# Query and key columns turned channel by token, their rotary partners swapped by transfers, and top-k rounds respaced

## The reference

```python
h = rmsnorm(x, norm_g)
a_q, a_k, a_v, a_z, i_q, i_k, i_w, b_q, b_k, b_v, b_z, b_o, b_i, b_f, g_a, g_b = split(h @ w_in)
q_a, k_a = partial_rope(a_q), partial_rope(a_k)     # 8 heads of 64 channels, the first 16 rotated
q_i, k_i = partial_rope(i_q), partial_rope(i_k)     # 16 query heads of 64, one key head
# branch a: 64-token chunks; top 128 keys of score = sum_h w_h * relu(q_i[h] . k_i / 8), then softmax attention
# branch b: chunked mLSTM on silu(causal_conv(b_q, b_k)), b_v, gates b_i and b_f, then head norm
x = x + (sigmoid(g_a) * y_a + sigmoid(g_b) * y_b) @ w_out
out = rmsnorm(x, final_norm_g)
# partial_rope: [x1*cos - x2*sin, x1*sin + x2*cos, rest], x1 and x2 the first and second 8 channels of a head
```

## Time and profile before

| | |
|---|---|
| median of 3 runs | 505.21 us (505.19 to 505.41) |
| the profiled execution's own time | 505.35 us |
| its span, first to last instruction | 503.6 us |
| granted TensorE clock, mean | 0.998 of full speed |
| TensorE matmul busy | 494.5 us, 98% |
| VectorE busy | 261.4 us, 52% |
| ScalarE busy | 239.2 us, 47% |
| GpSimd busy | 213.0 us, 42% |

### The profile page before, as it was taken

How to read it: one execution, slowest core, us unless ns; L and a number is a source line. 1 busy time by engine, 2 the same in 40 slices (tenths; PEclk the granted TensorE clock), 3 DMA queues, 4 the chain that set the end, 5 groups by cost and what they waited for, 6 DMA issues and landing times.

```text
span 503.6 us, 6823 instructions
## 1 busy us (share of the span) xinstructions
PE 494.5 (98%) x2518; PEld 411.6 (82%) x2518; DVE 261.4 (52%) x575; ACT 239.2 (47%) x434; POOL 213.0 (42%) x130
## 2 busy tenths in 40 slices
PE   8999999999999999999999999999999999999995
PEld 7688888888888888888788888888888888887885
DVE  3865777877899936525655567531111011125433
ACT  6757655555554455536568652413330333152322
POOL 0675131333344444247487451246534663373000
PEclk9999999999999999999999999999999999999999
DMA  8654432212343243112223112043234426453111
GB/s 284 188 153 128 126 87 79 84 48 80 83 111 99 85 117 104 52 43 85 57 70 85 43 43 65 20 125 104 62 87 125 126 58 193 126 149 144 42 55 72
DMA packets 44841, 48.94 MB, mean 97 GB/s; under 512 B 4996, under 2 KB 30212, under 8 KB 44808
## 3 DMA queue, kind: packets, MB, share of 16 engines
q1 hardware_dynamic: 43944, 47.65, 32.3%
q10 hardware_dynamic: 864, 0.86, 0.5%
HBM read 46.40 MB, written 2.11 MB: 96 GB/s over the span
## 4 chain that ended last, share of the span: by engine, by line
PE 94%; DMA 2%; SPq 1%; POOL 1%; ACT 1%; DVE 1%; issue 1%; DVEq 0%
PE pj L1486 24%; PE pj L1487 24%; PE pj L1488 24%; DMA w_raw<-in_w_in 2%; PE ob L1617 2%; PE tr L1606 2%; PE qb L1554 2%; PE qb L1553 2%; PE ob L1487 1%; PE qb L1487 1%; PE ob L1488 1%; PE qb L1488 1%; PE ob L1486 1%; PE qb L1486 1%; PE tr L1541 1%; PE qb L1601 1%
## 5 line engine op out<-in xcount | busy, mean ns | idle before, releaser
L529 POOL TENSOR_TENSOR w_lo<-w_raw,w_hi 128x1024 fp32r<-128x1024 f32 x70 | 168.9, 2424 | 156.3 <-ACT w_hi L875 156.0
L1486 PE MATMUL pj<-w_hi,h_hi 128*128 128x512 f32 x272 | 109.6, 403 | 0.0
L1488 PE MATMUL pj<-w_hi,h_lo 128*128 128x512 f32 x272 | 106.5, 392 | 0.0
L1487 PE MATMUL pj<-w_lo,h_hi 128*128 128x512 f32 x272 | 106.4, 391 | 0.0
L1486 PE MATMUL pj<-h_hi,w_hi 128*128 128x512 f32 (+1 forms) x200 | 78.1, 390 | 1.0 <-DVE h_lo L1129 1.0
L875 ACT ACTIVATE w_hi<-w_raw 128x1024 fp32r<-128x1024 f32 (+1 forms) x72 | 73.5, 1045 | 9.8 <-DMA w_raw<-in_w_out 6.3
L1488 PE MATMUL pj<-h_hi,w_lo 128*128 128x512 f32 (+1 forms) x200 | 77.9, 389 | 0.0
L1487 PE MATMUL pj<-h_lo,w_hi 128*128 128x512 f32 (+1 forms) x200 | 77.8, 389 | 0.0
L1488 PEld LDWEIGHTS pj<-w_hi,h_lo 128*128 128x128 f32 x272 | 51.1, 188 | 11.4
L1486 PEld LDWEIGHTS pj<-w_hi,h_hi 128*128 128x128 f32 x272 | 51.2, 188 | 8.3 <-issue 0.2
L1487 PEld LDWEIGHTS pj<-w_lo,h_hi 128*128 128x128 f32 x272 | 51.3, 188 | 8.0
(11 more groups left out here) (216 smaller groups left out, 817.3 us busy)
## 6 DMA issues: line engine op xcount, KB each, us to landing
w_raw<-in_w_in SPq DMA_DIRECT2D x60, 512.0 KB, 3.6
w_raw<-in_w_out SPq DMA_DIRECT2D x5, 512.0 KB, 3.5
x_tok<-in_x SPq DMA_DIRECT2D x4, 512.0 KB, 5.3
w_raw<-in_w_branch_a SPq DMA_DIRECT2D x8, 256.0 KB, 2.9
w_raw<-in_w_branch_b SPq DMA_DIRECT2D x8, 256.0 KB, 3.3
x_again<-in_x SPq DMA_DIRECT2D x1, 2048.0 KB, 9.3
w_late<-in_w_out SPq DMA_DIRECT2D x3, 512.0 KB, 6.1
out<-y_norm SPq DMA_DIRECT2D x4, 320.0 KB, 2.3
```

The source lines that it names most:

```text
L529: eng.tensor_tensor(lo[:, 0:m], raw_slot(n)[:, 0:m], hi[:, 0:m].bitcast(F32), ALU.subtract).then_inc(lo_by_dve if n in DVE_SLOTS else lo_b ...
L1486: pe.matmul(bank, a_hi, b_hi, start=first, stop=False)
L1487: pe.matmul(bank, a_hi, b_lo, start=False, stop=False)
L1488: return pe.matmul(bank, a_lo, b_hi, start=False, stop=last)
```

## The change

1. iq0, iq1, aq and ak are computed channel by token, as bq and bk were. The indexer groups have four units of 384 tokens instead of three of 128 tokens by 512 channels. The job `stage_chan` and its transposes are gone; ScalarE copies a unit to `iq_chan`, `q_a` or `k_chan`, and this copy alone frees the bank.
2. Rotation now works on whole channels by tokens. When a group's four units are out, ScalarE issues four transfers that copy rotary rows to their partners' places in `swapped` (`swap`); GpSimd multiplies that by the sines (`sin`), VectorE multiplies the channels by the cosines and adds the two (`turn`), block by block of 128 channels. Then ScalarE and VectorE make the two parts from SBUF (`parts`).
3. The tables come from the rope columns, which ride in `gate_l`, now 128 columns wide, through one transposition of four pieces (gate_rows); ScalarE copies them out four times. Rows are transposed back in four pieces (gate_cols). GpSimd blanks the padding at the start.
4. Scores go head by head, three tiles each. All 48 top-k rounds come after the last score: a round of tile 3 each 4.5 places from 66 on, the pair of tiles 2 and 1 two places behind it, to 135.

Places of the first units are now: iq0 4, iq1 20, aq 36, ak 52, bq 68, bk 84, bv 100, av 116, bo 132. Scores are at 28 to 65, attention starts at 139.

```diff
-UNITS = [("small", 0)] + [(g, j) for g in GROUPS for j in ((3, 2, 1) if g in ("iq0", "iq1") else range(TILES))]
+UNITS = [("small", 0)] + [(g, j) for g in GROUPS for j in range(TILES)]
-SCORES = [(i, h) for i in (3, 2, 1) for h in range(IDX_HEADS)]
+SCORES = [(i, h) for h in range(IDX_HEADS) for i in (3, 2, 1)]
-    return first_quarter("iq1") + 4 + (4 * s) // 5
+    return first_quarter("iq1") + 8 + (4 * s) // 5
...
-    for n, u in enumerate(STAGED):
-        put(4 * UNIT[u] + 4 + 2, "stage_chan", n)
+    for n, g in enumerate(TURNED):
+        end = first[g] + 16
+        put(end, "swap", n)
+        for b in range(KW):
+            put(end + 4 + 3 * b, "sin", 4 * n + b)
+            put(end + 5 + 3 * b, "turn", 4 * n + b)
+            if (g, b) in PARTS:
+                put(end + 6 + 3 * b, "parts", PARTS.index((g, b)))
...
-    start = score_place(IDX_HEADS - 1) + 1
-    place = start
+    start = score_place(len(SCORES) - 1) + 1
     for r in range(ROUNDS):
+        place = start + (9 * r) // 2
         at.setdefault(place, []).append((3, r))
-        place += 4 if first_quarter("ak") <= place < first_quarter("bq") else 2
-    pairs = place
-    for r in range(ROUNDS):
-        at.setdefault(pairs + 3 * r, []).append((2, r))
-        at.setdefault(pairs + 3 * r, []).append((1, r))
+        at.setdefault(place + 2, []).append((2, r))
+        at.setdefault(place + 2, []).append((1, r))
...
+            pool.memset(gate_l[:, :, :], 0.0)
+            pool.memset(two_rows[:, :], 0.0)
+            pool.memset(cos_t[:, :], 1.0)
+            pool.memset(sin_t[:, :], 0.0)
+            pool.memset(swapped[:, :], 0.0).then_inc(blank_made, 1)
...
+                    if job[0] == "sin":
+                        pool.wait_ge(swap_in, 64 * (job[1] // KW + 1))
+                        pool.tensor_tensor(swapped_rows(g, b), swapped_rows(g, b), table(sin_t, g), ALU.mult)\
+                            .then_inc(sin_made, 1)
...
+                elif kind == "swap":
+                    act.wait_ge(unit_out, UNIT[(g, KW - 1)] + 1)
+                    if n:
+                        act.wait_ge(rotated, KW * n)
+                    for first in (0, A_DIM):
+                        low, high = slice(first, first + HALF), slice(first + HALF, first + ROT)
+                        act.dma_start(swapped[low, 0:size], chan_flat(g)[high, :]).then_inc(swap_in, 16)
+                        act.dma_start(swapped[high, 0:size], chan_flat(g)[low, :]).then_inc(swap_in, 16)
+                elif kind == "parts":
+                    act.wait_ge(rotated, KW * TURNED.index(g) + b + 1)
                     for e in range(2):
-                        src, hi, _ = part(job, e)
+                        src, hi, _ = part(n, e)
                         act.activation(hi, src, ACT.Copy).then_inc(part_hi_made, 1)
...
+                elif kind == "turn":
+                    dve.wait_ge(swap_in, 64 * (m // KW + 1))
+                    dve.tensor_tensor(rows_b, rows_b, table(cos_t, g), ALU.mult).then_inc(cos_made, 1)
+                    dve.wait_ge(cos_made, m + 1)
+                    dve.wait_ge(sin_made, m + 1)
+                    dve.tensor_tensor(rows_b, rows_b, swapped_rows(g, b), ALU.add).then_inc(rotated, 1)
...
-                    if s in (0, 8, 24, 40):
-                        wait_read(pe, ("stage_chan", STAGED.index(("iq0" if h < 8 else "iq1", i))))
+                    if i == TILES - 1 and h % 2 == 0:
+                        pe.wait_ge(part_lo_made, h + 2)
...
-                        if g in CHAN_GROUPS:
-                            a, b = w_part(n, c + j * P, c + (j + 1) * P), h_part(k, 0, SEQ)
+                        wide = SEQ - first_token(g)
+                        if g in CHAN_GROUPS + TURNED:
+                            a, b = w_part(n, c + j * P, c + (j + 1) * P), h_part(k, SEQ - wide, SEQ)
-                        ins = three(bank[:, :], a, b, k == 0, k == KT - 1)
+                        ins = three(bank[:, 0:wide], a, b, k == 0, k == KT - 1)
```

207 lines of the change are left out of this document (108 added, 99 removed).

## The result

The changed kernel takes 532.05 us (median of 4 runs, 530.69 to 532.56) against 505.20 before: a ratio of 1.0526, 95% interval 1.0507 to 1.0546. The forecast was 520.5 us, in a range of 510 to 531. So the direction was right, but the time lies 1.05 us above the range, and the loss of 26.8 us is 11.5 larger than forecast. The profiled execution has 532.14 us and a span of 530.3.

A forecast was written before the change was run, and what follows sets the result against it. TensorE, busy 98%, was taken as the bound, with VectorE 95% full in bq and bk. 505.35 - 5.9 (saving) + 3.5 (first score) + 13.3 (queue) + 4.5 (port) = 520.85; forecast 520.5 us, range 510 to 531.

The forecast's parts named there:

- TensorE's saving: Whole TensorE queue: dropped transposes save 6.9 us, 384-column matmuls add 0.6, first unit 0.35; net gain 5.9 us.
- The full queue from the last score to bv: bq to bv: VectorE's fixed queue before unit 24's conv makes bv's second unit start 13.3 us late.
- sign of VectorE busy over 97%: From the last score (place 66) to bv: VectorE would show over 97% busy.
- The port waits: Last score to bv: two-SBUF-source VectorE instructions wait for GpSimd's running instruction; 4.5 us, bounds 0 and 22.
- nine pairs: Last score to bv: two-source instructions of 5 turns and 4 parts, each pair waiting 0.5 us for GpSimd.
- The scores stage: First score and the seven places after it: TensorE waits 3.5 us together, bounds 0.5 and 8.
- The first part of the term: First score: TensorE waits 2.8 us for swap transfers, GpSimd's remainder, sine product, sum and parts.
- another 0.7: Seven places after the first score: three turns, three parts and ten scores on VectorE cost 0.7 us more.
- rival D: TensorE's clock falls in the waits, mostly hidden in the stretch, three units not hidden; 524 to 537 us; chance 0.15.
- Rival B: VectorE's queue is the bound; port waits and first score cost almost nothing; 512.6 us, 510 to 513; chance 0.14.
- C: Faster: conv does not hold unit starts, as VectorE works ahead or rounds find gaps; 499.3 us; chance 0.10.

The follow-up runs named there:

- e14: Changed kernel without the rotation (swaps, sine products, turns) and without the top-k rounds; 501.16 us.
- e1: Changed kernel without all 96 top-k rounds, masks made from the raw scores; 523.96 us.
- e6: Changed kernel without top-k rounds, each turn's two two-source VectorE operations replaced by maxima of one SBUF source; 512.63 us.
- e17: Changed kernel without top-k rounds, swap transfers and sine products; each turn keeps two full-width one-source VectorE maxima; 506.66 us.
- e11: Changed kernel with GpSimd doing the whole rotation of aq and ak, every 4 places instead of 3; 533.67 us.
- e12: Changed kernel with swaps from SyncE's queue, scores by halves, aq and ak rotated on GpSimd, each tile's rounds spread up to its first use; 530.80 us.
- e13: Kernel before the change with only the new order: scores head by head, all rounds after the last score; 507.05 us.
- e15: Changed kernel with iq0's and iq1's turns alone using one-source maxima for their two-source VectorE operations; 524.65 us.
- e2: Changed kernel with all turns' two two-source VectorE operations replaced by maxima of one SBUF source and the same width; 519.88 us.
- e9: Changed kernel with each swap's four transfers issued from SyncE's queue instead of ScalarE's; 530.57 us.
- e8: Changed kernel with ak's jobs 22 places later, every 4; most parts two later; rounds spread to each tile's use; scores three later; 525.79 us.

## Why the forecast was too low, and what of it held

The forecast is 11.5 us short. 7.8 of them lie ahead of bq, in the term for the scores stage: that is the step that failed. 3.4 lie between bq and bv, in the size of the port waits. The sum itself has a slip that changes nothing: its terms make 520.75, not 520.85.

**TensorE's saving, 5.9: right.** e14 has bq 5.81 us early and bk, behind the last staged transposition of the kernel before, 6.30. Its one wait, of 1.65 us in bk, takes 1.9 of that back, so its time is 4.0 less and not 6. Matmuls of 384 columns run at the forecast pitch, 0.173 us in the median from iq0's start to aq.

**The full queue from the last score to bv, 13.3: right.** The forecast had 17.8 us of growth between bq and bv with the port waits, the trace has 21.2. TensorE was to wait 0, 1.9, 5.5 and 3.9 us at units 19 to 22, port waits apart; it waits 1.27, 3.86, 4.93 and 3.42. `conv` of unit 24 was to end 65 us after place 66 without port waits; it ends 72.4 after it (196.54, with place 66 at 124.07), and 8.0 us of port waits are in that. So the queue was counted well, and the port is what is missing. Its sign of VectorE busy over 97% is not met (63.06 of 67.90 us from 124.1 to 192, 93%), without harm: the rest is three waits of 0.7 us for ScalarE's first half and the small gaps between instructions.

What the sum leaves out is that the queue is not only long. In e1, without rounds, it has 30 us of room and TensorE still loses 12.9 us there (56.4 from bq to bv for 43.5 of matmuls); in e6, where the turns have one source as well, it loses 9.4, and in e17, without transfers and sine products, 6.8. By e1's waits it is ScalarE and VectorE that wait for each other. In the changed kernel VectorE is full and hides this; whoever relieves VectorE meets it next, as e11 and e12 did. That head-by-head scores give up the room is half of the reason: e13 has that order and those rounds and loses 2 us. The forecast's own prices agree, since without turns and parts they leave 49.4 us of its 63.4, and 51.7 are free. It takes both.

**The port waits, 4.5: the mechanism was right, the size not.** The sum counted nine pairs in the stretch at 0.5 us each. Its own factors, a chance of 0.55 and a wait of 1.2, make 0.66 a pair and 5.9 in all. There the two-source instructions took about 8.0 us longer than by themselves: aq's last turn alone 4.4, ak's second turn 2.4, parts 1.2. Taking the second source from aq's and ak's turns gives back 4.8 (e15 to e2). The forecast had queues that meet at random. The trace does not look like that, in two ways. Five times an instruction of a turn starts within 0.4 us behind a remainder (61.51 and 61.85, 95.07 and 95.19, 115.52 and 115.90, 125.68 and 125.71, 128.64 and 128.66) and pays nearly all of it. And where GpSimd has two sine products in a row, the sum is released by the end of the first and starts 0.15 us behind the second (46.80 and 46.95, 78.76 and 78.90, 111.43 and 111.57), so that it takes 0.7 to 1.0 us more. The second follows from the order of the jobs. That the first does too, because turns and the rounding of slots stand at fixed places, was argued, not tested; it is not the same turn in each group.

**The scores stage, 3.5: this is the term that failed.** Forecast was bq at 119.0, measured 126.82: with TensorE's saving taken off, 11.2 us are lost ahead of bq instead of 3.5. The first part of the term was good in size, a wait of 2.8 at the first score against 2.67, in part by luck: the transfers landed 1.0 us later than forecast, and the remainder ended 0.5 earlier. The second, "another 0.7", priced the three turns and three parts that follow, next to without port waits. The other seven turns and four parts ahead of the last score, those of iq1 and aq, were put at nothing, because the chain fits between swap and use; the term for the port counts only the nine pairs behind the last score. The trace has 13.2 us of port waits in turns and parts ahead of place 66. Four runs share out the 11.2 us by the start of bq:

| run | bq starts | adds |
|---|---|---|
| e14: no rotation, no rounds | 115.60 | |
| e17: + VectorE's own time in the turns | 116.37 | +0.8 |
| e6: + transfers and sine products | 119.80 | +3.4 |
| e15: second source in aq's and ak's turns, and rounds | 119.83 | +0.0 |
| after: + second source in iq0's and iq1's turns | 126.82 | +7.0 |

So the port waits of iq0 and iq1 are 7.0 us of it, and they are kept to the end (7.4 in the time). The way from VectorE to TensorE is ScalarE's queue: it waits 11.9 us in the scores stage for turns before its parts, 6.3 in e2, and the relus stand behind. Behind the wait of 2.01 us the clock falls as well, which the forecast had for bq and bk only.

**The clock (rival D): seen, small.** The time lies in D's range, 524 to 537, but not by D's way. Windows of 4 us behind the waits of 2.01, 3.86 and 3.42, the clock being the last number but two:

```profile
68.00:72.00 4.00, 4.00 (x16) 3.33 (x15) 1.85 (x3) 1.04 (x3) 1.61 (x1) 0.81 0.38 88
...
148.00:152.00 4.00, 3.27 (x8) 2.60 (x9) 3.97 (x3) 0.00 (x0) 4.00 (x3) 0.51 0.18 23
...
172.00:176.00 4.00, 3.24 (x8) 2.56 (x9) 3.83 (x10) 1.58 (x2) 3.22 (x2) 0.50 0.30 71
```

Full speed is 1.00 (2.4 GHz), 0.50 is 1.2 GHz. The Trainium skill, TensorE: Matmul & The Clock Gate, part 1, has the slow clock as the default that activity lifts, and the trace agrees in kind: behind these three waits and that of 4.93 us matmuls have a pitch of 0.43 for 2.5 us and more. Not every wait does it: behind the one of 2.67 us at 50.09 the windows up to 56 show 1.00, while in e1 the same wait was followed by 0.77, and behind e9's wait of 2.01 us the clock stays at 1.00. In bq and bk the slow matmuls delay units that would wait for `conv` anyway. VectorE's timeline shows it: none of the eight `conv` waits for its unit, and the last one ahead of bv's second unit, that of unit 24, is done before TensorE gets there:

```profile
194.31 2.32 DVE L1287 SCALAR_TENSOR_TENSOR conv_acc<-pj,conv_w_col,conv_acc 128x509 f32<-128x509 f32 x3
```

```profile
197.48 0.39 PE L1542 MATMUL pj<-w_hi,h_hi 128*128 128x512 f32 x1
```

`conv` ends at 196.63, unit 26 starts at 197.48 without a wait. So at most 0.9 us of the slow matmuls there reaches the end. In the scores stage the comparison with e9 puts them at 1.7 us or less. Mean clock over the span is 0.978.

**Rival B** (no port waits, 512.6) and **C** (faster, 499.3) did not come about. C's time is nearly what e14 gives, 501.16, once neither rounds nor turns are there.

**No better version.** Of the kernels that compute everything the best is still the one before. e8, the best with the channel layout, is 20 us above it. One way was not tried: gathering the rotated 32 rows of a group's four blocks into one compact tile, so that a group needs one product and one sum on VectorE.

## What to carry to other kernels

When work moves from an engine that reads PSUM to one that has both sources in SBUF, price each instruction with GpSimd's running one behind it, and ask whether both are released by the same event; here the turns took, in the mean of a group, 1.2 to 3 times their own length. In fixed queues follow each late instruction through the queue of the engine that waits for it: a turn late on VectorE held a part on ScalarE, and the part held the relus and copies for which TensorE waits. A saving on the bound engine is only there if the engine that gets the work has room in each stage, not on the average: VectorE was 52% busy before and 95% where it mattered.

## What the hardware showed that was not expected

- **The port wait shows on instructions with two SBUF sources; the others beside GpSimd keep their times.** `conv` (one source in PSUM) ran at 136.76 beside a remainder from 136.38 to 138.76 and took its usual 2.32 for three; MAX8 of one source took 0.56 beside a sine product (e2). The Trainium skill, GPSIMD Engine Reference, section 8 (Key points), says that VectorE's instructions with two SBUF inputs contend with GpSimd; the runs agree, and give the price: up to nearly the whole of GpSimd's running instruction, 2.64 us for one of 0.56 and 2.92 for one of 0.69. It works the other way too: in e12 a product of GpSimd that takes 1.28 us took 1.72 beside VectorE's parts.
- **A transfer of 8 rows costs ScalarE's queue more to issue than was forecast,** 0.63 to 0.66 us against 0.40 to 0.45, the first one 1.22; and from the last issue's start to the turn that waited for it went 3.95 us (40.58 to 44.53), against 2.6 forecast from the earlier trace rows.

```profile
38.00 1.22 ACTq L961 DMA_DIRECT2D swapped<-iq_chan  x1
39.25 0.64 ACTq L962 DMA_DIRECT2D swapped<-iq_chan  x1
39.92 0.63 ACTq L961 DMA_DIRECT2D swapped<-iq_chan  x1
40.58 0.63 ACTq L962 DMA_DIRECT2D swapped<-iq_chan  x1
```

- **The same wait is followed by either clock.** Behind a wait of 2.01 us the clock fell in the changed kernel and not in e9; behind one of 2.67 us it fell in e1 and not in the changed kernel.
